# Who issues the experts' second weights: SyncE, or ScalarE behind its split of a round's outputs

## The reference, cut to what matters

```python
def swiglu(x, w1, w3, w2):
    return (jax.nn.silu(x @ w1) * (x @ w3)) @ w2
# moe_ffn: 64 experts, 8 of them for each token
_, idx = lax.top_k(jnp.where(expert_mask, biased, NEG_INF), TOP_K)
...
def expert_block(args):
    toks, e, wts = args
    out = swiglu(xpad[toks], w1[e], w3[e], w2[e])
    return out * wts[:, None].astype(out.dtype)
...
return (routed + shared).reshape(B, S, D)
```

## Time and profile before

| | us |
|---|---|
| median of 3 runs | 1985.19 (1984.01 to 1992.59) |
| the profiled execution | 1986.75 |
| its span | 1984.8 |
| TensorE busy, share of the span | 1807.5, 91% |
| VectorE busy | 946.0, 48% |
| ScalarE busy | 358.2, 18% |
| SyncE's DMA queue, share of 16 engines' span | 581.47 MB, 74.4% |
| experts of layer 0, first products | from 372.88 |
| experts of layer 1, last first product | until 1650.9 |

### The profile page before, as it was taken

One profiled execution on the slowest core, in us unless ns is written; L12 is line 12 of the kernel. 1 busy time (PEld: TensorE's weight loads), 2 busy tenths in 40 slices (PEclk: granted clock), 3 DMA queues, 4 the chain that ended last, 5 costly groups with the idle time before them and its releaser, 6 DMA issues. The chain is left out here.

```text
span 1984.8 us, 27987 instructions
## 1 busy us (share of the span) xinstructions
PE 1807.5 (91%) x10545; PEld 1055.6 (53%) x10545; DVE 946.0 (48%) x2084; ACT 358.2 (18%) x699; POOL 44.1 (2%) x162
## 2 busy tenths in 40 slices
PE   6999999997987888899999989987897888999998
PEld 3847885443443333386588754443443434485485
DVE  2897665544343344369874354433343333451352
ACT  2133111011111111123231011111111112141131
POOL 1000001000000000000000000000000001010000
PEclk9999999999899899999999999999999899998999
DMA  9745777599999999966455648999999998333430
GB/s 346 262 168 188 276 280 274 216 375 421 420 421 420 419 420 420 408 217 221 170 195 207 256 157 353 418 421 420 421 420 421 421 420 314 113 123 107 161 107 22
DMA packets 146984, 586.39 MB, mean 295 GB/s; under 512 B 12844, under 2 KB 17568, under 8 KB 97440
## 3 DMA queue, kind: packets, MB, share of 16 engines
q1 hardware_dynamic: 145440, 581.47, 74.4%
q0 software_dynamic: 1408, 3.10, 0.6%
HBM read 583.49 MB, written 1.05 MB: 295 GB/s over the span
## 5 line engine op out<-in xcount | busy, mean ns | idle before, releaser
L1443 PE MATMUL banks<-weight_ring,x_units 128*32 128x512 f32 x2496 | 410.1, 669 | 92.4 <-DMA weight_ring<-in_w 92.4
L1443 PEld LDWEIGHTS banks<-weight_ring,x_units 128*32 128x32 f32 x2496 | 113.7, 122 | 261.6 <-issue 261.0
L2229 DVE TENSOR_TENSOR sig_h<-banks,sig_h 128x256 f32<-128x256 f32 x52 | 22.1, 425 | 400.8 <-ACT sig_h L1723 400.8
L1467 PE MATMUL banks<-slots,conv 128*32 128x512 f32 x800 | 181.4, 594 | 23.1 <-issue 20.2
L1092 PE MATMUL banks<-h_t,weight_ring 128*128 128x256 f32 x768 | 170.2, 380 | 0.1
L1443 PE MATMUL banks<-spare_slot,x_units 128*32 128x512 f32 x832 | 169.6, 592 | 0.0
L1092 PEld LDWEIGHTS banks<-h_t,weight_ring 128*128 128x128 f32 x768 | 145.2, 190 | 22.2 <-issue 1.6
L2508 PE MATMUL banks<-weight_ring,h_t 128*128 128x512 f32 (+2 forms) x384 | 134.0, 509 | 1.4 <-DVEq L2829 1.4
L1022 PE MATMUL banks<-h_t,weight_ring 128*128 128x256 f32 x512 | 111.5, 380 | 2.6 <-DVEq L1791 2.6
L1480 PE MATMUL banks<-o_parts,slot_of 128*128 128x512 f32 x416 | 110.7, 406 | 3.1 <-DVE o_parts L2266 3.1
L1443 PEld LDWEIGHTS banks<-spare_slot,x_units 128*32 128x32 f32 x832 | 55.7, 110 | 104.4 <-issue 104.0
(11 more groups left out here) (516 smaller groups left out, 2451.9 us busy)
## 6 DMA issues: line engine op xcount, KB each, us to landing
weight_ring<-in_w SPq DMA_DIRECT2D x204, 1024.0 KB, 14.0
weight_ring<-in_w_in SPq DMA_DIRECT2D x40, 2048.0 KB, 12.5
slots<-in_w SPq DMA_DIRECT2D x52, 1024.0 KB, 13.8
spare_slot<-in_w SPq DMA_DIRECT2D x48, 1024.0 KB, 17.1
weight_ring<-in_w_mod SPq DMA_DIRECT2D x20, 2048.0 KB, 12.4
qk<-in_w SPq DMA_DIRECT2D x26, 1024.0 KB, 18.7
h_t<-in_w SPq DMA_DIRECT2D x26, 1024.0 KB, 20.4
qk_t<-in_w SPq DMA_DIRECT2D x24, 1024.0 KB, 21.0
```

What stands on the lines that cost most here:

```text
L1443: mm = nc.tensor.matmul(h_bank[own, :], x_blk[:, i, k, own], w13(p % RING_X)[:, :, k, :], start=(k == 0), stop=(k == KT - 1), skip_group_c ...
L1467: mm = nc.tensor.matmul(o_banks[h][own, :], turned[:, i, f, own], w2_slots[p % RING_X][:, f, h * CHUNK:(h + 1) * CHUNK], start=(f == 0), s ...
L2229: v.tensor_tensor(act_pair, h_bank[:, 0:FF], sig_pair, ALU.mult)
```

## The change

SyncE's loop keeps the first weights alone. ScalarE gets the second weights of ranks 4 to 63: after `o_split(n - 1)`, and ahead of `sigmoid(n)`, it issues those whose slot round n - 1 has freed. These are ranks 4, 5 and 6 after round 0, 7 and 8 after round 1, 9 and 10 after round 2, 11 to 13 after round 3, and so on, up to 61 to 63 after round 23; three behind an odd round, two behind an even one. Each has a wait on the same semaphore as before, a read of the table and one DMA of 1 MiB. They go into ScalarE's own DMA queue. The second weights of ranks 0 to 3 stay with SyncE.

```diff
--- before.py
+++ after.py
@@ -929,21 +929,6 @@
                             expert13(l, held[p], p % RING_X)
                         else:
                             expert13_halves(l, held[p], p % RING_X)
-                        if FORMED < p < LAST - 1:
-                            load_second(at, held[p - 1], p - 1)
-                    for p in range(LAST - 2, N_EXPERTS):
-                        load_second(at, held[p], p)
-
-                def load_second(at, e, p):
-                    if p >= RING_X:
-
-                        sp.wait_ge(o_done, at(2 * NR, 2 * LAST_ROUND[p - RING_X] + 2))
-                        sp.sem_inc(wait_carrier, 1)
-                    else:
-
-                        sp.wait_ge(sh_done, at(T, T))
-                        sp.sem_inc(wait_carrier, 1)
-                    expert2(l, e, p % RING_X)
@@ -1735,6 +1720,23 @@
+                    def load_seconds(n):
+
+                        for p in range(FORMED, N_EXPERTS):
+                            s = p % RING_X
+                            if p < RING_X and n == 0:
+
+                                act.wait_ge(sh_done, at(T, T))
+                            elif p >= RING_X and n == LAST_ROUND[p - RING_X]:
+
+                                act.wait_ge(o_done, at(2 * NR, 2 * n + 2))
+                            else:
+                                continue
+                            act.sem_inc(wait_carrier, 1)
+                            e = act.value_load(K.table[0:1, FIRST_COL[p]:FIRST_COL[p] + 1], min_val=0, max_val=N_EXPERTS - 1)
+                            act.dma_start(w2_slots[s].rearrange("p f n -> p (f n)"),
+                                          A["w2"][ds(l, 1), ds(e, 1)].rearrange("a b (p f) n -> p (a b f n)", f=2)).then_inc(w2_filled[s], 16)
+
@@ -1749,6 +1751,7 @@
                         it, i = divmod(n, PAIRS)
                         if n > 0:
                             o_split(n - 1)
+                            load_seconds(n - 1)
                         sigmoid(n)
```

## The result

The changed kernel took a median of 1996.1 us (1991.43 to 2004.94, 10 runs), the kernel before beside it 1986.29 (1984.01 to 1994.92, 10 runs). The ratio is 1.0041, with an interval of 1.0025 to 1.0057: some 8 us slower, surely slower than before, and within the 0.5% that counts here as no change. Forecast: 1998.5 us, range 1979 to 2010. The profiled execution took 1997.74 us, 11.0 more than the profiled one of before.

The account below looks back on a forecast made before the run. The weight stream at its 420 GB/s ceiling was taken as the bound. Ramp, holes and tail summed to +6.3 us (layer 0) and +6.8 (layer 1), together +13 us: 1998.5 us against the 1985.19 us median, range 1979 to 2010.

Parts of the forecast that it names:

- ramp: Start of each layer's experts: one stream hole of 5.4 us (layer 1: 5.9) replaces holes losing 8.4; -3.0 and -2.5 us.
- holes in the middle: Full stretch of the experts: the queue runs nearly dry about five times per layer, 0.5 us each; +2.5 us per layer.
- tail: Last round of each layer: second weights overtake expert 63's first weights, delaying the second product; +6.8 us per layer.
- ScalarE's time: ScalarE after a round's outputs: two or three issues at 1.15 us each hide in 5.45 us of idle time; cost 0.
- Rival 4: ScalarE's issues cost over 1.8 us each, so even rounds' sigmoids come late: 25 us on top, 2023 us; chance 0.08.
- Halves: DMA queues of SyncE and ScalarE: with both at work, each gets half of the stream; 14 us hang on it.
- Rival 2: Loads served in order of issue: second weights keep their place, only a gain of 5.5 us at the start stays; 1980 us; chance 0.12.
- rival 3: Two queues carry more than one: full stretches at 433 GB/s shrink by 22.4 us; -15 us, 1970 us; chance 0.12.
- The swing: Odd rounds of the full stretch: outstanding loads go high and low in turn, about 9.5 and 2.5 us of stream.
- X' = 21 - X - f: Odd rounds: X us of loads outstanding at h_done and first product's length f give the next backlog X'; does not settle.
- rival 1: Odd rounds' backlog settles near 5.8 us, no holes: ramp -5.5, tail +12.6, so +7 us, 1992 us; chance 0.23.
- two cases of one tail: Last round: second product 6.4 us behind the stream's end with high backlog, 7.4 with low, at TensorE's pace; mean taken.

Follow-up runs that it names:

- kernel 4: Kernel before, with ScalarE's 120 waits and table reads added but no DMA there, SyncE issuing all loads as before: 1986.37 us, ratio 0.9991.
- kernel 3: Changed kernel's order of requests (each round's first weights, then second ones), but all issued by SyncE in one queue: 1984.98 us, ratio 0.9974 to the kernel before.
- kernel 5: Changed kernel, but ScalarE issues second weights of ranks 4 to 60 only, SyncE 61 to 63 as before: 1993.61 us, ratio 1.0022 to the kernel before.
- kernel 2: Changed kernel, but ScalarE issues second weights of ranks 61 to 63 only, SyncE the rest as before: 2004.62 us, ratio 1.0069 to the kernel before.
- kernel 8: Changed kernel, but SyncE issues all: by rounds (first, then second weights) up to rank 10, old order from 11: 1982.41 us, ratio 0.9960 to the kernel before.
- kernel 1: Changed kernel, but ScalarE issues second weights of ranks 4 to 10 only, SyncE the rest as before: 1982.25 us, ratio 0.9957 to the kernel before.
- kernel 6: Changed kernel, but ScalarE issues second weights of ranks 11 to 60 only, SyncE the rest as before: 1995.33 us, ratio 1.0028 to the kernel before.

## Why the prediction was right, point by point

Two sums per layer, in us. The ramp and the holes are each window's length times (1 - GB/s / 420), after less before; the tail is the second product's start behind the last landing, less the 0.1 of before.

| term | predicted | layer 0 | layer 1 |
|---|---|---|---|
| ramp | -3.0, -2.5 | 7.0 - 8.4 = -1.4 | 6.7 - 8.4 = -1.7 |
| holes in the middle | +2.5 | +0.9 | +1.8 |
| tail | +6.8 | 844.67 - 838.32 - 0.1 = +6.2 | 1667.99 - 1659.78 - 0.1 = +8.1 |
| sum | +6.3, +6.8 | +5.7 | +8.2 |

The rates are whole GB/s, which leaves the holes uncertain by some 0.4 us each. The last second product moved from 839.50 to 844.67 (+5.2) and in layer 1 from 1653.78 to 1667.99, 9.0 more than in layer 0. Of the 5.2, 1.5 us stood there before the experts (round 0's first product at 374.40 for 372.88): the experts themselves took 3.7 us longer in layer 0 and 9.3 in layer 1, for 5.7 and 8.2 in the table. Where the 2.0 and 1.1 us between them lie stays open. Together +14.2 us; the stretch behind it was 3.2 us shorter (327.8 for 331.0), which gives the +11.0 of the profiled executions. That stretch was between 327.7 and 334.1 us in the ten profiled kernels, among them those that change nothing near the end of a layer, so I take the 3.2 for scatter; it was not tried.

*ScalarE's time, 0.* Right: 1.12 us per issue for 1.15, the 5.45 us of idle time unchanged, and kernel 4 measures nothing. Rival 4 is out.

*The ramp.* One hole at the forecast place, and of the forecast size: 4.2 us of silence, 4 x (1 - 332/420) = 0.8 and 4 x (1 - 369/420) = 0.5 us until the stream is full, together 5.5 for 5.4. But the term was mis-sized, -1.4 and -1.7 for -3.0 and -2.5: it set the hole alone against the 8.4 us that whole windows had lost, and the stretch ahead of the hole, at 373 GB/s, loses another 13.8 x (1 - 373/420) = 1.5 us, which the prediction had taken as full from 383 on and left out before.

*Halves.* Right for the full stretch, 51.0 to 49.5% by the queues' own count, and wrong in the tail, where the prediction used it too: there SyncE had 34.2% against 65.7%, since its packets were half as large. The second queue's share is what carries the result: kernel 3 has the same order in one queue and none of the swing. Rival 2 is out by these rows (no order of issue), and rival 3 by the windows: 419 and 418 GB/s with both queues at work.

*The swing.* Its rule, X' = 21 - X - f, forecast high and low in turn, and so it came; but in the changed kernel it began small. Round 5 found 6.4 us outstanding (read from the landings) for the forecast 9, since its first product ran 9.6 us, not 7.1. The waits of rounds 5, 7 and 9 of layer 0 were 4.0, 5.0 and 3.5 us, those of 15 to 23 then 9.8, 0, 6.2, 1.4 and 9.4. In kernel 5, whose round 5 ran its 7.1 us and found 8.9 outstanding, the waits stood at 9.4 to 10.1 and 0 in turn from round 7 to round 21. A slope of -1 keeps a swing and does not damp it, so the end depends on how it starts. That the swing also grew in the changed kernel the rule gives only if f grows with the wait, as it did (7.05 us in round 17 after no wait, 9.56 in round 15 after 9.76); this was not tried by itself. Hence holes of 0.9 and 1.8 us for 2.5; rival 1 (the backlog settles) describes the first rounds and not the later ones.

*The tail.* Right in kind, off in size in layer 1: +8.1 for +6.8, by waits that the uneven shares would explain. There the wait in the middle of round 25's first product was 2.57 us, and its second half then ran 5.34 us where layer 0's ran 3.64 after a wait of 1.03; these 1.7 us are the difference. An estimate of what the uneven shares cost: when the first of rank 63's four loads of half a MiB had landed (826.94 and 1647.16), the other three were 1.57 MB; at half of 420 GB/s they would have landed 7.5 us later, at 834.4 and 1654.7, before TensorE asked for them (837.2 and 1657.3), and for 838.15 and 1659.78 as measured. So by this estimate the wait inside round 25, and the slower half product behind it, come from the small packets; it is not shown, since no kernel that loads rank 63 in large packets was run. TensorE's timeline of layer 1:

```profile
1659.82 5.34 PE L1428 MATMUL banks<-weight_ring,x_units 128*32 128x512 f32 x32 [2.57 <-DMA weight_ring<-in_w]
```

What the prediction treated as two cases of one tail, with its mean, are two mechanisms, and kernels 2 and 5 part them: overtaking with much outstanding (second product 9.6 and 9.1 us behind the stream, more than the forecast 6.4) and TensorE's pace behind a late round 23 (32.0 us from `h_done`, forecast 32.9; 4.4 and 4.6 us behind the stream for 7.4). By the traces they are alternatives and not a sum: less the 0.1 of before, 9.5 and 9.0 us of the one and 4.3 and 4.5 of the other would be 27.3 us, where the changed kernel lost 6.2 + 8.1 = 14.3. The times cannot tell: ramp, middle and tail alone are -0.43, +0.28 and +0.69%, together +0.54, and the whole change is +0.41, a difference within the intervals.

So the total, +13 us on 1985.19, was 8 to 10 us by the times and 11 by the profiled execution: the ramp gave half, the holes cost half of what was forecast, and the two errors nearly cancel. That the total came so close is luck in this part; that the tail outweighs the ramp is not. In the chances, slower by over 0.5% was given 0.49 and within 0.5% 0.39; it fell just inside the latter.

## What to carry to other kernels

Where a single queue already keeps the DMA engines full (420 GB/s at a share of 1.01), a second queue added no bandwidth here (418 and 419): it changes who is served first, and a load that nobody needs yet takes half of the stream, or two thirds where its packets are twice as large, from the one that the engine waits for. Moving a wait of 234 us off an issuing engine is worth at most what the DMA engines stood idle meanwhile, here 8.4 us per layer at the start of the experts, of which the change got back 1.4 and 1.7 and kernel 8 2.9; reorder the requests there, in the same queue, and leave the full stretch alone. The last loads before a serial point should land in the order in which they are used, since everything that TensorE does between the last first weight and the second product is paid in full.

## What was not expected of the hardware

TensorE can pay for a wait twice. After 9.76 us of waiting its first product's matmuls started at half the granted clock and rose within the product; windows of the changed kernel from 651.5 and from 657 us:

```profile
651.50:654.50 3.00, 2.99 (x16) 0.88 (x20) 0.00 (x0) 0.00 (x0) 0.00 (x0) 0.50 1.01 421
657.00:661.00 4.00, 4.00 (x41) 1.07 (x33) 0.00 (x0) 0.00 (x0) 0.00 (x0) 1.00 0.93 383
```

0.50 is the level of 1.2 GHz, 1.00 that of 2.4. The same 64 matmuls took 9.56 us here and 7.05 in the round that had not waited. Not every wait does this: of two rounds of layer 0 with nearly the same one, round 9 (3.49 us) took 9.87 us and round 13 (3.46 us) 7.07. In a full stretch this is hidden, since the stream sets the pace; in the last round of a layer it isn't, and it made the tail of kernel 2 some 2 us dearer than the prediction's case for it.

A steady alternation can come out of nothing but two queues, a ring of five slots and rounds of two and three experts: kernel 5 has it, kernels 1, 3 and 8, with one queue from rank 11 on, do not. It differs between two layers that run the same code. That its size is inherited from the first rounds, whose lengths vary with the clock, is how kernels 5, 6 and the changed one read, two layers each; no run set it on purpose.
